# Streaming the expert weights of a hybrid decoder layer in whole 4 MB matrices instead of 2 MB halves

## What is computed

```
def hier_moe(h, w_group, b_group, w_expert, b_expert, w_gate, w_up, w_down):
    ht = h.reshape(256, 2048)
    g_idx = argmax(ht @ w_group + b_group)              # 4 groups
    e_logits = (ht @ w_expert + b_expert)[group g_idx]  # 8 experts in the group
    top_val, top_idx = lax.top_k(e_logits, 2)
    gate = softmax(top_val) * softmax(g_logits)[g_idx]
    for each expert e, for the tokens x that chose it:
        hid = silu(x @ w_gate[e]) * (x @ w_up[e])       # 2048 -> 512, twice
        y  += gate * (hid @ w_down[e])                  # 512 -> 2048
```

## Time and profile before

| | us |
|---|---|
| median of 3 runs (lowest to highest) | 1449.82 (1449.28 to 1450.47) |
| the profiled execution | 1452.35 |
| its span on the core | 1450.4 |
| TensorE busy in matmuls | 1181.8 |
| VectorE busy | 610.6 |
| ScalarE busy | 217.4 |
| mean granted TensorE clock, of 2.4 GHz | 0.916 |

### The profile page before, as it was taken

One profiled execution on the slowest core, in us unless ns is written; L12 is line 12 of the kernel. 1 busy time (PEld: TensorE's weight loads), 2 busy tenths in 40 slices (PEclk: granted clock), 3 DMA queues, 4 the chain that ended last, 5 costly groups with the idle time before them and its releaser, 6 DMA issues.

```text
span 1450.4 us, 16131 instructions
## 1 busy us (share of the span) xinstructions
PE 1181.8 (81%) x6709; PEld 542.5 (37%) x6709; DVE 610.6 (42%) x1281; ACT 217.4 (15%) x460; POOL 15.5 (1%) x31
## 2 busy tenths in 40 slices
PE   6999999999999898967765877667775677768766
PEld 5885564565885552222121222112221112112222
DVE  4889999678453443322222222212221222212222
ACT  4211012373012411110000101000010000000001
POOL 4000000000000000000000000000000000000000
PEclk9999999999999989998877989978898898988888
DMA  9443452612547579999999999999999999999998
GB/s 295 151 147 133 142 203 109 220 63 87 174 174 269 218 275 396 427 429 426 428 428 427 428 427 429 426 427 428 428 427 427 429 427 427 428 429 425 427 427 318
DMA packets 74823, 478.82 MB, mean 330 GB/s; under 512 B 14917, under 2 KB 22469, under 8 KB 46208
## 3 DMA queue, kind: packets, MB, share of 16 engines
q1 hardware_dynamic: 73488, 477.45, 80.5%
q0 software_dynamic: 864, 0.25, 0.1%
q10 hardware_dynamic: 400, 0.10, 0.0%
HBM read 475.67 MB, written 2.11 MB: 329 GB/s over the span
## 4 chain that ended last, share of the span: by engine, by line
PE 51%; DMA 40%; DVE 4%; ACT 3%; issue 1%; SPq 1%; DVEq 0%; ACTq 0%
DMA late_ring<-in_moe_w_up_dram 18%; DMA ring<-in_moe_w_up_dram 17%; PE bank L691 10%; PE bank L1202 10%; PE bank L712 5%; PE bank L982 5%; PE bank L1162 4%; DMA late_ring<-in_moe_w_down_dram 3%; PE bank L1250 3%; PE bank L1237 2%; DMA ring<-in_w_in_dram 2%; PE bank L1092 2%; PE bank L973 2%; PE bank L1058 1%; ACT hT L1436 1%; PE bank L675 1%
## 5 line engine op out<-in xcount | busy, mean ns | idle before, releaser
L1202 PE MATMUL bank<-ring,x_gathered 128*32 128x512 f32 x1232 | 234.9, 698 | 104.2 <-DMA ring<-in_moe_w_up_dram 72.6
L2522 DVE TENSOR_TENSOR tokens_out<-tokens_out,bank 128x512 f32<-128x512 f32 x240 | 148.9, 682 | 405.9 <-PE bank L1250 405.9
L1202 PE MATMUL bank<-late_ring,x_gathered 128*32 128x512 f32 x816 | 171.9, 677 | 61.5 <-DMA ring<-in_moe_w_up_dram 32.8
L691 PE MATMUL bank<-ring,hT 128*128 128x512 f32 (+2 forms) x416 | 156.3, 536 | 3.3 <-ACT hT L1436 2.6
L1202 PEld LDWEIGHTS bank<-ring,x_gathered 128*32 128x32 f32 x1232 | 51.5, 122 | 226.0 <-issue 225.0
L1162 PE MATMUL bank<-x_tok,select 128*32 128x512 f32 x512 | 115.9, 1032 | 6.4 <-DVE select L2421 3.2
L691 PEld LDWEIGHTS bank<-ring,hT 128*128 128x128 f32 x416 | 78.6, 190 | 78.4 <-issue 67.0
L2477 DVE TENSOR_TENSOR x_gathered<-bank,gain_cols 128x512 f32<-128x512 f32 x32 | 22.1, 692 | 177.1 <-PE bank L1187 177.1
L1202 PEld LDWEIGHTS bank<-late_ring,x_gathered 128*32 128x32 f32 x816 | 37.3, 118 | 138.5 <-issue 136.9
L1250 PE MATMUL bank<-y_slots,weight_slots 32*128 32x512 f32 x496 | 82.4, 738 | 7.5 <-DVE tokens_out L2522 6.0
L1733 ACT ACTIVATE x_slots<-bank 128x512 f32<-128x512 f32 x32 | 19.1, 597 | 441.2 <-PE bank L1162 441.2
(11 more groups left out here) (436 smaller groups left out, 1164.2 us busy)
## 6 DMA issues: line engine op xcount, KB each, us to landing
ring<-in_moe_w_up_dram SPq DMA_DIRECT2D x36, 2048.0 KB, 42.7
ring<-in_moe_w_gate_dram SPq DMA_DIRECT2D x35, 2048.0 KB, 38.5
ring<-in_moe_w_down_dram SPq DMA_DIRECT2D x34, 2048.0 KB, 37.5
late_ring<-in_moe_w_down_dram SPq DMA_DIRECT2D x24, 2048.0 KB, 38.4
late_ring<-in_moe_w_up_dram SPq DMA_DIRECT2D x23, 2048.0 KB, 43.1
late_ring<-in_moe_w_gate_dram SPq DMA_DIRECT2D x23, 2048.0 KB, 38.0
ring<-in_w_in_dram SPq DMA_DIRECT2D x20, 1024.0 KB, 9.0
ring<-in_w_out_dram SPq DMA_DIRECT2D x16, 1024.0 KB, 5.8
```

The lines of the kernel that those rows point to most:

```text
L691: mm = pe.matmul(b, lhs(i)[:, P * tt:P * tt + P], piece_view(key)[:, c, at:at + cols], start=i == 0, stop=i == n - 1)
L1202: mm = pe.matmul(gu_bank[SLOTS * c:SLOTS * c + SLOTS, :], XGT[:, at, n % 4, n // 4, :], pieces[c % 2][:, FF * (n % 8):FF * (n % 8) + FF], ...
L2522: ins = v.tensor_tensor(y, x, mix[c][:, :], ALU.add)
```

## The change

Gate, up and down of an expert are each moved by one transfer of 4 MB whose rows are 32 KB (`whole`), for experts 2 to 31 except the parts named below. The ten places are paired into five doubles (`moe_double`); gate's double holds what were pieces q0 and q2, up's q1 and q3, down's q4 and q5 (`places_of`). Each double has its own semaphores (`head_in`, `main_in`). SP waits for a double until its former matrix is wholly used (`freed`): gate and up until the fourth quarter, down until its second half. TensorE's waits stand in the same places of its order, but each wait is now for a whole matrix. Experts 0 and 1 are still loaded in pieces, into other places (`FILL`); the gate of expert 2 comes in four transfers of 1 MB, and the last piece of expert 1 (`LONE`) after expert 2's up. In the loop SP waits for the fourth quarter before both gate and up. The last expert's gate and up still come as first half, then quarters, its down as half and two quarters. Rows of down are numbered `(p h k)` instead of `(h p k)`, so `turn_hidden` reads its operand with a step of 4 elements instead of 2.

```diff
-SLOT_ORDER = (3, 7, 9, 4, 8, 0, 1, 2, 5, 6)
-SPLIT = 2
+FILL = {8: 0, 9: 1, 0: 2, 1: 3, 4: 4, MOE_RING: EXTRA, 2: 6, 3: 7, 6: 8, 7: 9, 5: 10}
+LONE, LONE_AT = 11, 4
+DOUBLES = (4, 0, 1, 3, 2)
+STREAM = 2
+HEAD_LOADS = 3 * (MAIN - STREAM)
+LOOP_DOUBLES = [DOUBLES[(HEAD_LOADS - 3 + q) % 5] for q in range(3)]
+MAIN_DOUBLES = [DOUBLES[(HEAD_LOADS + k) % 5] for k in range(5)]
+MAIN_LOADS = 3 * (N_EXP - MAIN - 1)
+def freed(n, first):
+    return PPE * (first + n // 3) + (PPE if n % 3 == 2 else 4)
+def places_of(doubles):
+    g, u, d = doubles
+    return [2 * g, 2 * u, 2 * g + 1, 2 * u + 1, 2 * d, 2 * d + 1]
...
+            def whole(e, q, d, arrived):
+                sp.dma_start(moe_double(d).rearrange("p (k n) -> p k n", k=KD if q < 2 else GC),
+                             whole_source(e, q)).then_inc(arrived[d], 16)
...
-                for r in range(SPLIT):
-                    expert_half(piece_of(MOE_RING + r), h)
-            for r in range(MOE_RING + SPLIT, ring_no(HEAD_PIECES)):
-                sp.wait_ge(head["pieces_done"], piece_of(r - MOE_RING) + 1)
-                expert(piece_of(r))
+                for k in (4 * h, 8 + 4 * h):
+                    a = FF * k
+                    sp.dma_start(moe_double(DOUBLES[0])[:, a:a + PIECE].rearrange("p (k n) -> p k n", k=4),
+                                 whole_source(STREAM, 0)[:, k:k + 4, :]).then_inc(head_in[DOUBLES[0]], 16)
+            sp.wait_ge(head["pieces_done"], 4)
+            whole(STREAM, 1, DOUBLES[1], head_in)
+            sp.wait_ge(head["pieces_done"], 5)
+            expert(LONE, LONE_AT)
+            for n in range(2, HEAD_LOADS):
+                if n < 5:
+                    sp.wait_ge(head["pieces_done"], (8, 10, 12)[n - 2])
                 else:
+                    sp.wait_ge(head["pieces_done"], freed(n - 5, STREAM))
+                whole(STREAM + n // 3, n % 3, DOUBLES[n % 5], head_in)
...
-                for q in range(PPE):
-                    sp.wait_ge(head["pieces_done"], tally(i, PPE, q + 1))
+                for q in range(3):
+                    sp.wait_ge(head["pieces_done"], tally(i, PPE, 4 if q < 2 else PPE))
...
-            for g in range(MOE_RING, MAIN_PIECES):
-                sp.wait_ge(main["pieces_done"], g - MOE_RING + 1)
-                main_expert(g)
+            for n in range(2, MAIN_LOADS - 3):
+                sp.wait_ge(main["pieces_done"], freed(n - 2, 0) if n < 5 else freed(n - 5, 1))
+                main_load(n)
```

More of the change, by code:

```diff
@@ L460, in moe_slot, with moe_double @@
             return late[:, a:a + WIDE]
+        def moe_double(d):
+            w = ring if d < RING // 4 else late
+            a = (d if d < RING // 4 else d - RING // 4) * 2 * WIDE
+            return w[:, a:a + 2 * WIDE]
         def shape4(ap, q):
@@ L542, in _ @@
                     wait_filled(sp, "wo01")
-                    expert(EXTRA)
+                    expert(EXTRA, MOE_RING)
                 if key == ("wo1", PAIRS[0][1]):
@@ L603, in _ @@
-            for g in range(PPE, MOE_RING):
-                sp.wait_ge(head["pieces_done"], HEAD_PIECES - MOE_RING + g - PPE + 1)
-                main_expert(g)
+                for k in (4 * h, 8 + 4 * h):
[3 more added lines that the diff above has]
+            sp.wait_ge(head["pieces_done"], 4)
@@ L606, in _ @@
+            for n in range(2):
+                sp.wait_ge(head["pieces_done"], freed(HEAD_LOADS + n - 5, STREAM))
+                main_load(n)
             sp.wait_ge(s["tables"], 1)
@@ new lines, in _ @@
+            for n in range(2, MAIN_LOADS - 3):
+                sp.wait_ge(main["pieces_done"], freed(n - 2, 0) if n < 5 else freed(n - 5, 1))
+                main_load(n)
+            sp.wait_ge(main["pieces_done"], freed(MAIN_LOADS - 7, 1))
+            g, u, d = (MAIN_DOUBLES[(MAIN_LOADS - 3 + q) % 5] for q in range(3))
+            for q, a in ((0, g), (1, u)):
+                sp.dma_start(moe_slot(2 * a).rearrange("p (k n) -> p k n", k=8),
+                             whole_source(N_EXP - 1, q)[:, 0:8, :]).then_inc(main_in[a], 16)
@@ new lines, in _ @@
+            for q, a in ((0, g), (1, u)):
+                for h in range(2):
+                    k = 8 + 4 * h
+                    sp.dma_start(moe_slot(2 * a + 1)[:, PIECE * h:PIECE * h + PIECE].rearrange("p (k n) -> p k n", k=4),
+                                 whole_source(N_EXP - 1, q)[:, k:k + 4, :]).then_inc(s["tail_high" if h else "tail_low"], 16)
+            sp.wait_ge(main["pieces_done"], freed(MAIN_LOADS - 6, 1))
+            w = whole_source(N_EXP - 1, 2)
+            sp.dma_start(moe_slot(2 * d).rearrange("p (k n) -> p k n", k=GC), w[:, :, 0:1024]).then_inc(main_in[d], 16)
@@ L618, in _ @@
+            for c in range(2):
+                sp.dma_start(moe_slot(2 * d + 1)[:, PIECE * c:PIECE * c + PIECE].rearrange("p (k n) -> p k n", k=GC),
+                             w[:, :, 1024 + 512 * c:1536 + 512 * c]).then_inc(s[("tail_quarter", "tail_down")[c]], 16)
             stores = (("last_added", 2, 0, 512), ("last_added", 4, 512, 512), ("last_copied", 1, 1024, 256),
@@ L1361, in _, with arrived_head @@
             for j in range(FIRST):
-                place = [place_of(PPE * j + q) for q in range(PPE)]
-                def arrived_head(slot, j=j, place=place):
-                    return arrived_first(PPE * j + place.index(slot))
+                if j < STREAM:
+                    place = [LONE_AT if g == LONE else FILL_AT[g] for g in range(PPE * j, PPE * j + PPE)]
+                else:
+                    place = places_of([DOUBLES[(3 * (j - STREAM) + q) % 5] for q in range(3)])
+                def arrived_head(slot, j=j):
+                    if j == 1 and slot == LONE_AT:
+                        return wide_in[slot], 48
+                    if j < STREAM:
+                        return wide_in[slot], 16 if slot == MOE_RING else 32
+                    d = slot // 2
+                    uses = len([n for n in range(3 * (j - STREAM) + 3) if DOUBLES[n % 5] == d])
+                    return head_in[d], 16 * uses + (48 if d == DOUBLES[0] else 0)
                 straight(head, j, FIRST - 1, place, arrived_head)
@@ L1380, in _ @@
                         turn_weights(head, i)
-                    gate_up(head, i, n, 1, arrived_late, LOOP_SLOTS[2 * (n // 2):2 * (n // 2) + 2])
+                    gate_up(head, i, n, 1, arrived_late, late_place[2 * (n // 2):2 * (n // 2) + 2])
                 turn_hidden(head, i)
-                down(head, i, arrived_late, LOOP_SLOTS[4:6])
+                down(head, i, arrived_late, late_place[4:6])
                 for tt in range(TT):
```

97 lines of the change are left out of this document (35 added, 62 removed).

## The result

| | before | after |
|---|---|---|
| median in one comparison, us (lowest to highest, runs) | 1452.04 (1449.28 to 1456.43, 16) | 1456.56 (1450.84 to 1460.73, 16) |
| ratio to before, 95% interval | | 1.0028 (1.0017 to 1.0039) |
| the profiled execution, its span | 1452.35, 1450.4 | 1458.79, 1456.7 |
| TensorE busy, mean granted clock | 1181.8, 0.916 | 1237.4, 0.907 |

The ratio is + 4.0 us on 1450; it is the one recorded for the comparison, and the quotient of the two medians is slightly another (4.5 us). The forecast of 1450.3 was less than the 0.2% that can be told from no change; the outcome is slower by more than that, and still inside the forecast's range of 1446.5 to 1457.0.

The account below looks back on a forecast made before the run. The weight stream was taken to set the pace: 8.5 us saved by longer rows, 7.4 lost at expert 9, net + 0.5 at the end, giving span 1450.9 and median 1450.3 us; range 1446.5 to 1457.0.

Parts of the forecast that it names:

- The bound and its chain: Whole kernel: the weight stream sets the pace; the question is when TensorE starts the last expert, with 28.8 us following.
- Expert 9: At the loop's seam the queue runs dry, since the next transfer waits for all four quarters; loss 7.4 us.
- Every expert later, free of charge: Each expert starts 9.8 us later against the stream, but the queue has 10.1 us to spare; no loss.
- Rival 3: The queue runs dry at every expert because quarters run at 1.2 GHz; + 14 us, 1464; chance 0.05.
- The pace: Stream up to expert 30's up: longer rows save 0.10 us in each of 85 transfers of 4 MB, 8.5 us.
- Rival 1: Long rows save little, 0.03 us or less per transfer, at 428 GB/s; 1456 to 1459, taken as 1457; chance 0.24.
- long rows are cut up again: Weight transfers: the lower bound of the pace term, where the saving for each 4 MB transfer is 0.
- Small edits: Fewer SP issues and turn_hidden's step of 4: 0 to 55 ns on 8 loads, 0 to 1.3 us, taken as 0.
- The start of the stream: Restart and first experts: same bytes at the same releases, TensorE waits about 8 us but the queue stays fed; nothing lost.
- The end: Experts 30 and 31: TensorE now late, starting 2.2 us later, 1.7 us back from a faster first quarter; net + 0.5 us.
- Rival 2: The pause at expert 9 evens out the DMA engines; up to some 4 us come back, 1446.5; chance 0.13.

Follow-up runs that it names:

- e5: The changed kernel with each 4 MB matrix moved as two transfers of 2 MB with rows of 16 KB; ratio to before 1.0053.
- e11: The changed kernel with up of expert 10 issued after the loop and ScalarE's write sorted into pairs (turn_hidden step 2); ratio to before 0.9968.
- e7: The changed kernel with up of expert 10 issued after the loop and down's rows numbered as before (16 KB, step 2); ratio to before 0.9984.
- e9: The changed kernel itself, unaltered, measured a second time; ratio to before 1.0043.
- e3: The changed kernel with up of expert 10 issued after the loop, behind expert 9's matrices; ratio to before 0.9992.
- e12: The changed kernel with only ScalarE's write sorted into pairs, so turn_hidden reads with a step of 2; ratio to before 1.0014.
- e10: The changed kernel with ScalarE's fully sorted write (turn_hidden step 1), measured a second time; ratio to before 1.0038.
- e4: The changed kernel with ScalarE's write fully sorted, so turn_hidden's weight loads are contiguous, 32 KB rows kept; ratio to before 1.0024.
- e8: The kernel before with the four matmuls of turn_hidden issued twice over, still with a step of 2; ratio to before 1.0004.
- e1: The changed kernel with down's rows numbered as before (16 KB rows, turn_hidden step 2), still 4 MB transfers; ratio to before 1.0022.

## What held in the prediction and what did not, step by step

- **The bound and its chain: right.** The stream sets the pace; the time is decided by when expert 30 starts and how long two experts last.
- **Expert 9: right.** Landing forecast 797.96, measured 797.87; issue 812.5, measured 812.08; down of expert 10 at 824.7, measured 824.21; restart cost 2.5, measured 2.4. The hit of the first is partly luck: in this execution R came 4.0 us before that of before, and the start of the stream lost as much. The loss of 7.4 us was 6.9 and 6.1 by the landings in the two profiles of after, 5.7 to 7.5 in all seven with the old order, and 7.0 by four pairs of ratios.
- **Every expert later, free of charge: right.** Between 830 and 1400 us the queue ran dry in no profile. Rival 3 falls.
- **The pace: right in kind, 0.03 us for each matrix too large.** The term was 85 x 0.10 = 8.5; it is 85 x 0.07 = 6.0. It was half of the 0.22 us that 4 MB lose from rows of 16 KB to rows of 8 KB, as for a cost that hangs on the number of rows. The 0.22 itself was read from rounded rows: in the three profiles with the places of before, the landings of the four 1 MB transfers are 2.48 to 2.52 us apart, so that 4 MB take 9.96 to 10.00 against 9.79, and half of that loss is 0.09 to 0.10. The records of single packets in the traces bear out the kind: one row is one packet, also at 32 KB, and its median is 162, 313, 613 and 1215 ns for rows of 4, 8, 16 and 32 KB, 11 to 13 ns less for each two rows made one. For the eight rows that an engine is spared in 4 MB this gives 0.09 us, and the landings show 0.07; where the rest goes stays open. The page's figure (the Trainium skill, DMA: Bandwidth & Descriptors, Why small descriptors are slow), an estimated 3.5 ns for a packet or 0.03 us for each 4 MB, is too low by both. The fit of 2.0 us plus bytes over 436 GB/s, quoted beside it, is given there (the Trainium skill, the same page, Anatomy of one DMA) for transfers that GpSimd issues; these come from SP, and it had no part in the sum. Rival 1 (nothing saved) falls by e5, and its "long rows are cut up again" by the packets.
- **Small edits: the step that failed.** This term was put at 0, and the step of 4 was bounded by 0 to 55 ns a load, from a comparison of `turn_hidden` at 2 with `turn_rows` at 1. These are loads of different groups; with a step of 1 `turn_hidden` itself takes 191 ns. The comparison said nothing on the step, and the bound was not one. The load went up by 131 ns, and the eight matmuls by 0.92 us; on the path in experts 30 and 31, 1.8 us. The Trainium skill (SBUF — State Buffer, Door 1: The DMA port swizzle) says that SBUF gives full rate while at least two accesses fall into one line of 16 bytes. The loads at steps of 1, 2 and 4 elements of 4 bytes agree, as does ScalarE's copy written in order, in pairs and as single elements, 0.60, 0.63 and 1.04 us. By that rule the edit from 2 to 4 crosses the edge, and the term would not have been 0. The same note of the Trainium skill gives 4 float32 as the distance of stride that is free; read as a step of 4 that differs from the 327 ns here, and the measurement decides.
- **The lower clock behind it: not foreseen.** Rival 3 spoke of four quarters at 1.2 GHz, and put against it that after the first quarter every expert runs at full clock. That was not so even before: 7 of its 31 downs took 5.10 to 5.29 us, at a granted clock of 0.68 to 0.71. In the first profile of after such a down cost 2.7 us in expert 30, where nothing hides it. One of those before, timeline of TensorE:

```profile
1056.32 5.15 PE L1237 MATMUL bank<-ring,hidden 128*32 128x512 f32 x32 [1.01 <-DVE hidden L2514]
```

- **The start of the stream, "nothing": wrong in some executions**, by 0.6 to 4.5 us where the step of 4 and transfers of 4 MB meet, and right in all seven profiles of 4 MB transfers without it. Its cause is inferred from which profiles show it, not isolated.
- **The end: the sum was right for its conditions.** From the landing of up of expert 30 to the end it gave 1450.9 - 1400.8 = 50.1 us; e11 and e7, which have no step of 4, show 50.1 and 49.7. With 1.8 more it is 51.9 (e9: 51.6, e3: 52.0), and with the slow down as well 54.6 (after: 54.8). A down can be slow there without the step of 4 too: in e12 it took 5.08 us and in e10 4.96, with ends of 51.7 and 52.4. The 52.3 of e4 holds 1.4 us more than e9 and e10 behind TensorE's last instruction.
- **Rival 2 (the pause evens the engines out): refuted.** Before, from 819.87 to 1401.92 us, 118 pieces took 582.05 us, 4.8 more than 118 x 4.892; after, from 824.21 to 1401.90, 59 matrices took 577.7, 4.8 more than 59 x 9.71.

Put together: saving short by 2.5, `turn_hidden` + 1.8, pause 0.5 to 1.3 less, and 0.6 to 7.2 from the start of the stream and the slow down. On the forecast of + 0.5 that is + 4.1 to + 11.5 from R, before interruptions that differ by some 2 us; the two profiles have + 3.8 and + 10.4 over that of before, the ratios + 4.0 and + 6.2.

That the range held this time is partly luck. Its upper half was there for rival 1, a stream that saves nothing, and that did not happen. What came instead, a smaller saving, the eight matmuls of `turn_hidden` at 2.05 us and the losses that come with slow downs in some executions, all point the same way, and the forecast had only the first of them among its cases.

## What to carry to other kernels

When an edit renumbers rows, look at who reads the result with what step, and price that step from the same instruction at another step, not from a neighbour of the same shape; then ask if the group lies on the path anywhere, because a stream hides such a cost in 28 experts and shows it in the last two. A larger unit of transfer needs a larger unit of free space: wherever the order of issue has a seam, as at the loop, count the bytes that are still queued when the first wait after it can be met. Cut a profile at a landing or an event that both kernels share before comparing spans.

## What the runs showed of the hardware that was not expected

- A weight load of 128x128 in float32 from SBUF takes 191, 196 and 327 ns at steps of 1, 2 and 4 elements (means of 256 in e4, e12 and after); ScalarE's copy of 128x512 takes 597 ns in order, 625 in adjacent pairs, 1038 as single elements 128 apart.
- Behind a 2.05 us group of strided loads down runs at a lower granted clock in most experts (over 5 us in 93 of 155; 0.58 in the stretch above), behind an equally long group of denser loads it mostly does not (7 of 31, e8).
- Again and again two landings come late, some 1.3 to 1.9 us together, and the pair returns after 182 to 215 us (207 in the mean in before: after 730.3 and 755.6, 932.4 and 962.7, 1144.4 and 1169.7, 1351.4 and 1376.8), whatever the size of the transfers and with the pause or without. In the packet records of before, some 30 times between 640 and 1400 us, two packets in a row, the second starting as the first ends, take 1.0 to 1.2 us each instead of 0.61. That these make the landings late fits, but is not shown.
- One row is one packet up to 32 KB, and a packet has a median of 162, 313, 613 and 1215 ns for 4, 8, 16 and 32 KB.
- Rows of 32 KB instead of 16 KB raise the stream from 428 to 431 GB/s (e5 against after); a transfer twice as large with the same rows does not (the downs of e1 and e7).
